# A transformer block's cross attention run between the tiles of its projections, squares added on VectorE, and three program blocks joined

## The reference

```python
h = h + merged @ w_out
a, m = rmsnorm(h, norm_cross_g), rmsnorm(mem, norm_mem_g)      # mem: 256 x 1024
q = (a @ w_q).reshape(b, t, 4, 256)
kk, vv = jnp.split(m @ w_kv, 2, axis=-1)                        # 4 heads of 256 each
p = jax.nn.softmax(einsum('bthd,bmhd->bhtm', q, kk) * 256 ** -0.5)
h = h + einsum('bhtm,bmhd->bthd', p, vv).reshape(b, t, 1024) @ w_o
h = h + peer_ffn(rmsnorm(h, norm_ffn_g), w_peer_q, ...)         # 128 of 16384 experts a token
...
x = x + rms_norm(hybrid_mixer(...) , post)                      # second block
g = dwconv3(hn @ w_gate, conv_w, conv_b)                        # D_FF = 2816
x = x + rms_norm((gelu(g) * (hn @ w_up)) @ w_down, post)
```

## Time and profile before

| | |
|---|---|
| median of 3 runs | 3315.23 us (3314.86 to 3315.61) |
| the profiled execution | 3316.35 us |
| its span, first to last instruction | 3314.4 us |
| TensorE busy | 3103.0 us (94%) |
| VectorE, ScalarE, GpSimd busy | 1893.8, 1111.8, 1113.8 us |
| mean granted clock of TensorE | 0.967 of full speed |

### The profile page before, as it was taken

One profiled execution on the slowest core, in us unless ns is written; L12 is line 12 of the kernel. 1 busy time (PEld: TensorE's weight loads), 2 busy tenths in 40 slices (PEclk: granted clock), 3 DMA queues, 4 the chain that ended last, 5 costly groups with the idle time before them and its releaser, 6 DMA issues. The chain is left out here.

```text
span 3314.4 us, 38011 instructions
## 1 busy us (share of the span) xinstructions
PE 3103.0 (94%) x14826; PEld 1563.4 (47%) x15096; DVE 1893.8 (57%) x2841; ACT 1111.8 (34%) x1611; POOL 1113.8 (34%) x522
## 2 busy tenths in 40 slices
PE   8899988999798999999999999999998888988997
PEld 4344455445644546464665444444443345433443
DVE  6764996432333858777671355555554853378721
ACT  4334254423332334243433333333333432323221
POOL 1223411333323342434333444444442320224432
PEclk9899999999999999999999999999999987999999
DMA  4212211222122345656567655555552210112321
GB/s 154 96 58 76 102 39 39 89 102 96 70 94 78 134 153 153 197 156 197 153 187 215 229 203 203 203 203 203 204 203 77 96 57 26 58 57 89 108 96 64
DMA packets 265873, 415.84 MB, mean 125 GB/s; under 512 B 148024, under 2 KB 148216, under 8 KB 265312
## 3 DMA queue, kind: packets, MB, share of 16 engines
q1 hardware_dynamic: 265696, 413.40, 37.2%
HBM read 341.56 MB, written 69.22 MB: 124 GB/s over the span
## 5 line engine op out<-in xcount | busy, mean ns | idle before, releaser
L736 POOL TENSOR_TENSOR weights_lo<-weights_as_loaded,weights_hi 128x1024 bf16<-128x1024 f32 x503 | 1112.5, 2214 | 2161.1 <-ACT weights_hi L732 2161.1
L732 ACT ACTIVATE weights_hi<-weights_as_loaded 128x1024 bf16<-128x1024 f32 x507 | 533.2, 1054 | 1263.6 <-PE banks L672 485.6
L2172 DVE TENSOR_TENSOR activation_lo<-activation_f,activation_hi 128x512 bf16<-128x512 f32 x128 | 279.2, 2181 | 312.6 <-ACT activation_hi L2064 312.6
L2033 PE MATMUL banks<-activation_hi,weights_hi 128*128 128x512 bf16 x1004 | 380.6, 379 | 1.1
L2033 PE MATMUL banks<-activation_hi,weights_lo 128*128 128x512 bf16 x1003 | 380.2, 379 | 1.1
L2033 PE MATMUL banks<-activation_lo,weights_hi 128*128 128x512 bf16 x1003 | 380.2, 379 | 1.1
L1985 PE MATMUL banks<-normed_lo,weights_hi 128*128 128x512 bf16 x999 | 378.6, 379 | 1.8
L1985 PE MATMUL banks<-normed_hi,weights_lo 128*128 128x512 bf16 x1000 | 379.0, 379 | 1.3
L1985 PE MATMUL banks<-normed_hi,weights_hi 128*128 128x512 bf16 x991 | 376.3, 380 | 1.2
L2050 ACT ACTIVATE gelu_out<-banks 128x512 f32<-128x512 f32 x128 | 76.2, 596 | 423.4 <-PE banks L1985 416.2
L2155 DVE TENSOR_TENSOR one_hot_b<-iota,pick_column 128x1024 bf16<-128x1024 bf16 x64 | 129.0, 2016 | 144.4 <-PE banks L2006 143.2
(11 more groups left out here) (495 smaller groups left out, 4937.3 us busy)
## 6 DMA issues: line engine op xcount, KB each, us to landing
weights_as_loaded<-in_u_tiles SPq DMA_DIRECT2D x128, 512.0 KB, 3.8
weights_as_loaded<-in_v_tiles SPq DMA_DIRECT2D x128, 512.0 KB, 3.5
gelu_of_dots<-gelu_out SPq DMA_DIRECT2D x128, 256.0 KB, 2.2
activation_f<-gelu_of_dots SPq DMA_DIRECT2D x128, 256.0 KB, 3.8
expert_weight<-expert_weights SPq DMA_DIRECT2D x128, 256.0 KB, 4.0
expert_weights<-weight_grid_even SPq DMA_DIRECT2D x32, 512.0 KB, 4.7
expert_weights<-weight_grid_odd SPq DMA_DIRECT2D x32, 512.0 KB, 5.6
weights_as_loaded<-in_w_xbc SPq DMA_DIRECT2D x24, 512.0 KB, 3.4
```

What stands on the lines that cost most here:

```text
L732: self.nc.scalar.activation(self.whi[:, s, :], self.wraw[:, s, :], ACT.Copy).then_inc(self.w_hi[s], 1)
L736: self.nc.gpsimd.tensor_tensor(self.wlo[:, s, :], self.wraw[:, s, :], self.whi[:, s, :], ALU.subtract).then_inc(self.w_lo[s], 1)
L2033: ins = nc.tensor.matmul(self.ps[:, c, :], v[:, j, c * P:(c + 1) * P], g[:, n % 4, :], start=n + m == 0, stop=n == NV - 1 and m == 2)
L2172: nc.vector.tensor_tensor(glo[:, j, :], gf[:, j, :], ghi[:, j, :], ALU.subtract).then_inc(S["g_lo"], 1)
```

## The change

- `Split` and `Sums` add the squares of the chunks on VectorE (`add`) into the first square, and TensorE sums once (`pe`), after the last add. 57 adds in seven norms (one of them the memory's, with 256 columns).
- Block ends go: all stages from the input x to peer_q are one block; w_out2, ffn_gate, ffn_up and ffn_down are one block.
- The order becomes w_out, cross_k, cross_v, cross_q. The load of the memory waits for w_out's input to be done, as it takes over memory of the stage before.
- cross_v is made in tokens: the memory chunk is the stationary side, the weight moves in 512 columns, four banks (4 to 7) accumulate over four units, and ScalarE scales by a column of one over root. `to_tokens` goes.
- `CrossAttention` has each head's steps as methods. Heads 0 to 2 are put behind the tiles of cross_q, head 3 and the end of head 2 inside the first four units of cross_out.
- The gelu of tile o is done behind tile o + 2 of ffn_gate on ScalarE. ffn_up's product goes through `few_chunks`, ScalarE rounds it and VectorE subtracts; both parts lie in the place of the gate's tile.
- The stage semaphores of both former blocks are cleared once, after peer_q.

```diff
         if c >= 4:
-            act.wait_ge(self.summed, self.s0 + c - 3)
-        self.nc.scalar.activation(self.sq[:, c % 4, 0:self.tok], self.x[:, c, :], ACT.Square).then_inc(self.squared, 1)
+            act.wait_ge(self.added, self.a0 + c - 3)
+        self.nc.scalar.activation(self.square(c), self.x[:, c, :], ACT.Square).then_inc(self.squared, 1)
...
-    def pe(self, pe, c):
-        pe.wait_ge(self.squared, self.q0 + c + 1)
-        self.nc.tensor.matmul(self.k.ps[:, self.bank, 0:self.tok], self.k.ones, self.sq[:, c % 4, 0:self.tok],
-                              start=c == 0, stop=c == self.nch - 1).then_inc(self.summed, 1)
+    def add(self, dve, c):
+        dve.wait_ge(self.squared, self.q0 + c + 1)
+        if c:
+            if c > 1:
+                dve.wait_ge(self.added, self.a0 + c - 1)
+            self.nc.vector.tensor_tensor(self.square(0), self.square(0), self.square(c), ALU.add).then_inc(self.added, 1)
+
+    def pe(self, pe):
+        pe.wait_ge(self.added, self.a0 + self.nch - 1)
+        self.nc.tensor.matmul(self.k.ps[:, self.bank, 0:self.tok], self.k.ones, self.square(0), start=True, stop=True
+                              ).then_inc(self.summed, 1)
...
+class CrossAttention:
...
+    def scores(self, pe, h):
+        S = self.S
+        pe.wait_ge(*self.q_ready[2 * h + 1])
+        if h:
+            pe.wait_ge(S["exped"], h)
+        else:
+            pe.wait_ge(S["v_taken"], 4)
+        for t in range(TT):
+            for d in range(2):
+                ins = self.nc.tensor.matmul(self.ps[:, self.SCORES + t // 2, t % 2 * MEM:(t % 2 + 1) * MEM],
+                                            self.qT[:, 2 * h + d, t * P:(t + 1) * P], self.kT[:, 2 * h + d, :], start=d == 0,
+                                            stop=d == 1)
+        ins.then_inc(S["scored"], 1)
+
+    def turn(self, pe, h):
+        S = self.S
+        pe.wait_ge(S["normed"], h + 1)
+        if h:
+            pe.wait_ge(S["stored"], 2 * h)
+        for m in range(2):
+            for t in range(TT):
+                ins = self.nc.tensor.transpose(self.ps[:, self.TURNED + m, t * P:(t + 1) * P],
+                                               self.prob[:, h % 2, t, m * P:(m + 1) * P], self.k.ident)
+            ins.then_inc(S["turned"], 1)
+
+    def values(self, pe, h):
+        S = self.S
+        pe.wait_ge(S["copied"], 2 * h + 2)
+        for d in range(2):
+            for m in range(2):
+                at = h * MD + d * P
+                ins = self.nc.tensor.matmul(self.ps[:, self.TURNED + d, :], self.v[:, m, at:at + P], self.pT[:, m, :],
+                                            start=m == 0, stop=m == 1)
+            ins.then_inc(S["valued"], 1)
...
+    def store(self, dve, h):
+        S = self.S
+        for d in range(2):
+            dve.wait_ge(S["valued"], 2 * h + d + 1)
+            hi, lo = (o[:, 2 * h + d, :] for o in self.out)
+            self.nc.vector.tensor_copy(hi, self.ps[:, self.TURNED + d, :]).then_inc(S["hi"], 1)
+            dve.wait_ge(S["hi"], 2 * h + d + 1)
+            self.nc.vector.tensor_tensor(lo, self.ps[:, self.TURNED + d, :], hi, ALU.subtract).then_inc(S["stored"], 1)
...
-        def late_sums(pe, c):
-            if c >= 5:
-                split.pe(pe, c + 8)
-
         k.project("ssd", io["w_ssd_branch"], DC, 2, y2, times(gate), "dve", nxt=io["w_out"], normed=split.waits,
-                  scaled=split.scaled, within=late_sums, after={"dve": merge, "act": merge_hi})
+                  scaled=split.scaled, after={"dve": merge, "act": merge_hi, **last_sum(split)})
         k.run(dve=lambda dve: merge_rest(DC - 1))
-    s2.close()
...
+        def load_mem(sp):
+            sp.wait_ge(*multiplied)
+            sp.wait_ge(merged_lo, DC)
+            sp.dma_start(memT[:, :, :], io["memT"]).then_inc(mem_in, 16)
+
+        k.run(sync=load_mem, dve=lambda dve: dve.wait_ge(mem_in, 16))
+        k.project("w_out", io["w_out"], DC, 1, k.aT, plus(k.hT), "dve", nxt=io["w_cross_k"],
                   normed=lambda c: ((merged_hi, c + 1), (merged_lo, c + 1)), after=split_beside(split, msplit))
         split_end(split, msplit)
-        k.project("cross_q", io["w_cross_q"], DC, 1, raw, scaled_to(cq, k.rs), "dve", nxt=io["w_cross_k"],
-                  normed=split.waits, scaled=split.scaled, after=last_sum(split, msplit))
         k.project("cross_k", io["w_cross_k"], DC, 1, mem2, scaled_to(ck, mem_rs[0]), "dve", nxt=io["w_cross_v"], tok=MEM,
-                  normed=msplit.waits, scaled=msplit.scaled)
-        k.project("cross_v", io["w_cross_v"], DC, 1, mem2, scaled_to(cvT, mem_rs[0]), "dve", nxt=io["w_cross_out"], tok=MEM)
-    s3.close()
-    mix.close()
-    k.zero_semaphores()
-    k.to_tokens(cvT, DC, cv, 2)
-    k.cross_attention(cq, ck, cv, k.aT)
-    s2.close()
-
-    s2 = ExitStack()
-    s3 = ExitStack()
-    pq = k.sb("peer_query", [P, 2 * PH, T], ctx=s3)
-    s4 = ExitStack()
-    raw = k.pair("raw", [P, DC, T], ctx=s4)
-    with k.together():
+                  normed=msplit.waits, scaled=msplit.scaled, after=last_sum(split, msplit))
+        stream = Stream(k, [(io["w_cross_v"], DC)], io["w_cross_q"])
...
+        def v_pe(pe):
+            pe.wait_ge(split.root, split.r0 + 1)
+            pe.wait_ge(msplit.root, msplit.r0 + 1)
+            for u in range(DC):
+                slot = stream.ready(pe, u)
+                half, pair = u // 4, u % 4
+                for n in range(2):
+                    for m in range(2):
+                        for a, w in ((0, k.whi), (1, k.whi), (0, k.wlo)):
+                            ins = nc.tensor.matmul(k.ps[:, 4 + 2 * half + m, :], mem2[a][:, 2 * pair + n, m * P:(m + 1) * P],
+                                                   w[:, slot, n * 512:(n + 1) * 512], start=pair == 0 and n == 0 and a == 0 and w is k.whi,
+                                                   stop=pair == 3 and n == 1 and w is k.wlo)
+                stream.multiplied(ins, u)
...
+        def q_dve(o, _):
+            if o in (2, 4, 6):
+                h = o // 2 - 1
+                if h:
+                    cross.store(nc.vector, h - 1)
+                cross.maxima(nc.vector, h)
+                cross.normalize(nc.vector, h)
+
+        def q_act(o, _):
+            if o in (2, 4, 6):
+                cross.exps(nc.scalar, o // 2 - 1)
+            if o in (3, 5, 7):
+                cross.copies(nc.scalar, o // 2 - 1)
+
+        def q_pe(o, emptied):
+            q_ready[o] = emptied
+            if o in (4, 6):
+                cross.values(nc.tensor, o // 2 - 2)
+            if o in (2, 4, 6):
+                cross.scores(nc.tensor, o // 2 - 1)
+            if o in (3, 5, 7):
+                cross.turn(nc.tensor, o // 2 - 1)
+
+        k.project("cross_q", io["w_cross_q"], DC, 1, raw, scaled_q, "dve", nxt=io["w_cross_out"],
+                  normed=split.waits, scaled=split.scaled, after={"dve": q_dve, "act": q_act, "pe": q_pe})
+
+        def last_dve(dve):
+            cross.store(dve, 2)
+            cross.maxima(dve, 3)
+            cross.normalize(dve, 3)
+            cross.store(dve, 3)
...
+        def last_head(pe, c):
+            if c == 1:
+                cross.values(pe, 2)
+                cross.scores(pe, 3)
+            if c == 3:
+                cross.turn(pe, 3)
+            if c == 5:
+                cross.values(pe, 3)
...
-        k.project("cross_out", io["w_cross_out"], DC, 1, k.aT, plus(k.hT), "dve", nxt=io["w_peer_q"],
-                  after=split_beside(split))
+        k.project("cross_out", io["w_cross_out"], DC, 1, k.aT, plus(k.hT), "dve", nxt=io["w_peer_q"], outer=True, within=last_head,
+                  normed=lambda c: ((cross.S["stored"], c + 1),), after=split_beside(split))
...
+        def gate_act(o, _):
+            if 4 <= o < 12:
+                again.act(nc.scalar, o - 4)
+            if o >= 2:
+                gelu(o - 2)
+
...
-    with k.together():
-        k.scalar_pass(ff, ff, ACT.Gelu_apprx_tanh)
-        k.project("ffn_up", io["ffn_w_up_2"], FC, 1, k.aT, times(ff), "dve", nxt=io["ffn_w_down_2"],
-                  after=k.then_dve(split_hidden))
...
+        def hidden(me, o, bank, j):
+            nc.vector.wait_ge(gelued, o + 1)
+            return nc.vector.tensor_tensor(k.few[:, o % 4, :], bank, chunk(ff, o), ALU.mult)
+
+        def hidden_act(o, emptied):
+            nc.scalar.wait_ge(*emptied)
+            nc.scalar.activation(ff2[:, o, 0, :], k.few[:, o % 4, :], ACT.Copy).then_inc(hidden_hi, 1)
+
+        def hidden_rest(o):
+            nc.vector.wait_ge(hidden_hi, o + 1)
+            nc.vector.tensor_tensor(ff2[:, o, 1, :], k.few[:, o % 4, :], ff2[:, o, 0, :], ALU.subtract).then_inc(hidden_lo, 1)
+
+        def last_gelus(act):
+            for o in (FC - 2, FC - 1):
+                gelu(o)
+
+        k.run(act=last_gelus)
+        k.project("ffn_up", io["ffn_w_up_2"], FC, 1, k.aT, hidden, "dve", nxt=io["ffn_w_down_2"],
```

(2 more changed lines are left out.)

379 lines of the change are left out of this document (191 added, 188 removed).

## The result

The changed kernel takes 3236.55 us (median; 3234.72 to 3237.22), the kernel before 3315.05 us beside it: a ratio of 0.976 (0.975 to 0.978), 78.5 us faster. The forecast was 3230.7 us, its range 3218 to 3247. The direction, the range and the size of the large terms were right; the sum was 6 us too hopeful. The profiled execution took 3236.03 us, its span 3234.2.

A forecast was written before the change was run, and what follows sets the result against it. TensorE is busy nearly all the time, so it must execute less or wait less. Gains of 53.5 us (first part) and 31.0 (second), together 84.5, take the median 3315.23 to 3230.7 us; range 3218 to 3247.

The forecast's parts named there:

- 12.9 + 9.0 + 6.0 + 6.0: Gains in us from fewer f32 sums: z and ssd, w_out and cross_q, after cross_out, second feed-forward's pre-norm.
- rival (a): VectorE's adds fall into GpSimd's operations in seven tiles, costing 12 us, 3243; chance 0.13.
- ssd into w_out: Block end between these stages goes, with its idle time and lower clock: gain 7.7 us.
- cross_k's waits: At cross_k's start, new stalls of 1.7 and 2.9 us, plus 2.6 us of lower clock: loss 7.2 us.
- rival (b): In cross attention, GpSimd holds each head's chain and TensorE waits at each turning: 8.4 us, 3239; chance 0.12.
- Rival (c): cross_k's stalls overlap, no clock is lost, cover holds elsewhere: 9 us less, 3222; chance 0.12.
- (d): Rival: f32 sums' time returns as waits for weights or VectorE, only block ends gain: 3274; chance 0.04.
- (e): Rival: short waits keep TensorE at 1.2 GHz in the merged block from w_out's end to peer_q: 3391; chance 0.03.
- The stall behind the burst: In w_out2, three sums between the burst and the fifth tile go: gain 2.7 us.
- the tail: At w_out2's end, grows by an add less what the table load hides: 0.5 us.
- Gate into up: Between ffn_gate and ffn_up, 9.23 us idle and 2.6 of lower clock become a 2.6 us wait: gain 9.2 us.
- No clock is lost on 2.6: At ffn_up's start, TensorE's wait of 2.6 us for a bank brings no lower clock.

The follow-up runs named there:

- the two half kernels: Kernel before with only the VectorE adds of squares, 3275.78 us; kernel after with those adds undone, 3274.75 us.
- the last experiment: Kernel after with four edits and the keys' load ahead of the clears, plus ScalarE rounding weights before emptying banks in w_out2's first four units: 3217.94 us.

## Why the prediction was right, and where it was off

**Sums of squares.** Right in size. With the adds alone TensorE's busy time falls by 48.5 us and the kernel gains 38.4; of the 33.9 us of 12.9 + 9.0 + 6.0 + 6.0 the trace shows 21.1 + 5.3 + 5.3 = 31.7. In z and w_out every add of 512 columns takes 0.68 us, so rival (a) falls. Ten of the 57 adds did meet GpSimd and took 1.35 to 2.62 us (three in cross_out, four in w_out2, three in ffn_down); TensorE waited for one of them, the last of w_out2.

**ssd into w_out, cross_k, attention.** Right, to 29.1 for 28.3 us (0.8 of it by chance, ahead of the change) and 29.9 for 28.9. cross_k's waits (3.8 for 4.6 us) and clock (2.8 for 2.6) were close, and undoing them gave 6.3 to 6.9 us for 7.2. No head is waited for: rival (b) falls, though its margin was under 0.1 us. Rival (c) falls with the clock that did fall, (d) with the two half kernels, and (e) with a granted clock of 1.00 in the windows from 765 to 860 us.

**Clearing semaphores.** Right in after (3.86 for 3.7 us), and the cause is shown by dealing the clears out and by the clears themselves, which stand in the trace 0.057 us apart (0.059 in the prediction).

**w_out2: 1.4 instead of 4.8 us.** The stall behind the burst shrank by 2.6 us as forecast. Two steps failed. I priced the lost cover at its length alone: before, three f32 sums stood in the gap and the clock held (1.00 from 2870 to 2878 us); without them a wait of 1.99 us is followed by nine matmuls at 1.2 GHz, 1.7 us. That this was the clock's loss, and that it hangs on this gap, the last experiment shows. And I put the tail at 0.5 us, with the add at 0.69; it fell into GpSimd's last operation and took 2.19, so that the tail grew by 2.0. Taking this add off the tail gave 1.8 us back. The row that priced it stood in the text, 2.49 us; I had timed the collision for w_out and not for the end of w_out2.

**Pre-norm: 5.3 instead of 6.0.** VectorE kept up. The lower clock behind the wait at ffn_gate's start lasted longer: 13 matmuls in 5.48 us in after, 10 in 4.10 before, which is the 0.7 us. The two stretches, after first:

```profile
2851.84:2857.30 5.46, 5.24 (x12) 1.93 (x14) 5.39 (x9) 2.95 (x5) 0.00 (x0) 0.50 0.00 0
```

```profile
2908.80:2912.80 4.00, 3.57 (x9) 1.46 (x11) 3.93 (x7) 2.38 (x4) 0.00 (x0) 0.50 0.00 0
```

**Gate into up: right by luck, then 2.5 us short.** I took VectorE's lag at the gate's end from the kernel before. But the gelus that I had called "beside the gate's units on ScalarE, which has room" bind ScalarE's rounding, and through it GpSimd, to VectorE's third step: the lag grew to 4.96 us, which cost 2.4. That it comes with the moved gelus and not with the adds two kernels show: with the adds alone the bank is empty 2.56 us after TensorE's last matmul of the gate, as before, and with all but the adds TensorE waits 4.95 us. Hidden in the same row of the table is a gain that I hadn't counted: ffn_gate itself is 2.4 us shorter, since four small waits, which cost 2.8 us, became one of 0.6. "No clock is lost on 2.6" was moot at 4.96: 13 matmuls took 5.36 us for 2.81, so 2.5 us were lost, about as much as before. The block end before ffn_down and ffn_down itself came out at 11.2 (11.3 less the 0.1 us by which ffn_up's clock loss is smaller than before's) for 11.0.

The missing 4.3 us of the profile (84.5 forecast, 80.2 measured) are thus the clock behind three waits (1.7 + 0.7 + 2.5), the w_out2 tail (1.5 more) and the gate's lag (2.4), together 8.8, against 2.4 in the gate, 0.2 behind ffn_up and 2.1 ahead of w_out2; 0.2 us are left over.

## What to carry to other kernels

Work that is taken from an engine may be the cover of a wait: look at each gap it leaves, and price the clock behind the gap besides the gap. When an operation moves to an engine that is waited for in a ring, follow who waits for whom round the ring; a spare share of busy time doesn't say that two engines won't meet in every tile. And when an edit gains three times what it should, or nothing of a wait that did shrink, compare starts of the same instructions and the granted clock stretch by stretch: the part that lies where the edit isn't can be taken back by the next edit.
